# Expert stage of a two-block model: one gather of token rows for two turns, and weight slots handed over in parts

## The reference, cut to what matters

```python
T, D, N_EXPERTS, D_EXPERT, TOP_K = 256, 1024, 32, 512, 2
grp_prob = softmax(hf @ w_group_router + b_group_router)
grp_p, grp_idx = top_k(grp_prob, 1)
exp_logits = (hf @ w_expert_router + b_expert_router).reshape(T, 4, 8)
top_p, top_i = top_k(softmax(exp_logits[grp_idx]), TOP_K)
gates = grp_p * top_p / sum(top_p)
...
def expert_block(xb, e):                 # xb: the rows of the tokens that chose expert e
    hid = silu(xb @ w_expert_gate[e]) * (xb @ w_expert_up[e])
    return hid @ w_expert_down[e]
...
y = segment_sum(yb * row_gate[:, None], row_tok)   # back to the tokens
x = x + y
```

## Time and profile before

| what | us |
|---|---|
| median of 3 runs | 1495.97 |
| the profiled execution, its own time | 1494.68 |
| its span, first to last instruction | 1492.9 |
| first matmul of the first expert turn | 1040.04 |
| last matmul of y in the last turn ends | 1485.97 |

### The profile page before, as it was taken

One profiled execution on the slowest core, in us unless ns is written; L12 is line 12 of the kernel. 1 busy time (PEld: TensorE's weight loads), 2 busy tenths in 40 slices (PEclk: granted clock), 3 DMA queues, 4 the chain that ended last, 5 costly groups with the idle time before them and its releaser, 6 DMA issues.

```text
span 1492.9 us, 20008 instructions
## 1 busy us (share of the span) xinstructions
PE 1444.0 (97%) x7734; PEld 1031.3 (69%) x7734; DVE 638.8 (43%) x1074; ACT 545.6 (37%) x814; POOL 448.6 (30%) x305
## 2 busy tenths in 40 slices
PE   8999999999999999999999999998999899999998
PEld 7788888888788888887878689855454354454453
DVE  6673644446663645434358555644112121212111
ACT  6666544345666534335455421212111111111111
POOL 2472545444463554447679030100000000000000
PEclk9999999999999999999999999999999999999999
DMA  7341454554341454556863601038999999999995
GB/s 270 128 163 57 150 218 170 198 191 142 130 161 58 165 203 169 208 187 202 268 226 104 227 6 57 2 133 374 374 428 428 428 428 428 422 416 422 427 421 242
DMA packets 44675, 351.89 MB, mean 236 GB/s; under 512 B 5187, under 2 KB 7151, under 8 KB 20015
## 3 DMA queue, kind: packets, MB, share of 16 engines
q1 hardware_dynamic: 43758, 349.35, 60.3%
q10 hardware_dynamic: 720, 1.20, 0.2%
q0 software_dynamic: 112, 0.17, 0.1%
HBM read 347.78 MB, written 1.07 MB: 234 GB/s over the span
## 4 chain that ended last, share of the span: by engine, by line
PE 73%; DMA 10%; issue 6%; DVE 5%; ACT 2%; POOL 2%; DVEq 1%; SPq 1%; POOLq 0%; ACTq 0%
PE psum L1743 12%; PE psum L1055 10%; PE psum L1057 10%; PE psum L1056 10%; DMA ring<-in_w_expert_up 9%; PE psum L1347 8%; PE psum L1769 5%; PE psum L1349 4%; PE psum L1045 3%; PE psum L1695 2%; PE psum L1704 1%; PE psum L1176 1%; DMA weights_raw<-in_second_w 1%; PE psum L1562 1%; POOL weights_split L896 1%
## 5 line engine op out<-in xcount | busy, mean ns | idle before, releaser
L896 POOL TENSOR_TENSOR weights_split<-weights_raw,weights_split 128x512 fp32r<-128x512 f32 (+2 forms) x253 | 395.9, 1597 | 360.9 <-ACT weights_split L1844 360.9
L1844 ACT ACTIVATE weights_split<-weights_raw 128x2048 fp32r<-128x2048 f32 (+4 forms) x154 | 243.5, 1586 | 254.6 <-PE psum L1057 150.3
L1743 PE MATMUL psum<-ring,arena 128*64 128x512 f32 x960 | 224.2, 593 | 10.9 <-DMA ring<-in_w_expert_up 9.8
L1347 PE MATMUL psum<-h_split,weights_split 128*128 128x512 f32 x512 | 181.2, 398 | 1.4 <-DVE weights_split L896 1.4
L1743 PEld LDWEIGHTS psum<-ring,arena 128*64 128x64 f32 x960 | 72.9, 137 | 139.8 <-issue 139.8
L1055 PE MATMUL psum<-weights_split,h_split 128*128 128x512 f32 (+3 forms) x400 | 152.0, 380 | 6.3 <-POOL weights_split L896 4.8
L1055 PE MATMUL psum<-weights_split,hidden_split 128*128 128x512 f32 (+1 forms) x384 | 151.4, 394 | 0.0
L896 DVE TENSOR_TENSOR weights_split<-weights_raw,weights_split 128x2048 fp32r<-128x2048 f32 (+3 forms) x53 | 119.5, 2259 | 71.3 <-ACT weights_split L1844 69.4
L1057 PE MATMUL psum<-weights_split,h_split 128*128 128x512 f32 (+3 forms) x400 | 149.9, 375 | 0.0
L1056 PE MATMUL psum<-weights_split,h_split 128*128 128x512 f32 (+3 forms) x400 | 149.8, 374 | 0.0
L1057 PE MATMUL psum<-weights_split,hidden_split 128*128 128x512 f32 (+1 forms) x384 | 148.1, 386 | 0.0
(11 more groups left out here) (379 smaller groups left out, 1928.9 us busy)
## 6 DMA issues: line engine op xcount, KB each, us to landing
weights_raw<-in_layer_w SPq DMA_DIRECT2D x94, 1024.0 KB, 4.8
arena<-in_w_expert_down SPq DMA_DIRECT2D x32, 2048.0 KB, 13.4
ring<-in_w_expert_up SPq DMA_DIRECT2D x32, 2048.0 KB, 16.9
ring<-in_w_expert_gate SPq DMA_DIRECT2D x28, 2048.0 KB, 16.3
weights_raw<-in_second_w SPq DMA_DIRECT2D x44, 512.0 KB, 5.2
arena<-in_w_expert_gate SPq DMA_DIRECT2D x3, 2048.0 KB, 9.5
weights_raw<-in_layer_w SPq DMA_DIRECT2D x6, 768.0 KB, 4.2
ring<-in_w_out SPq DMA_DIRECT2D x2, 2048.0 KB, 17.2
```

Source lines behind the costliest of these rows:

```text
L896: ins = eng.tensor_tensor(W.part(j, 1, n)[:, cols], W.raw(j, n)[:, cols], W.part(j, 0, n).bitcast(F32)[:, cols], ALU.subtract)
L1347: pe.matmul(both.rearrange("p (w s) -> p w s", w=2), w[0][:, k, f * P:(f + 1) * P], hTp[:, :, k, :], start=(k == 0), stop=False)
L1743: ins = pe.matmul(bank[half(j), :], xe[h][:, k, half(j)], w[j][:, k, :], start=(k == 0), stop=(k == KD - 1))
L1844: act.activation(W.part(j, 0, w), W.raw(j, w), ACT.Copy).then_inc(W.hi, 1)
```

## The change

What it does, part by part:

- **Gather.** The normalised rows are kept as two rounded parts, `rows_high` (written by ACT, in the place of `xn2`) and `rows_low` (a new DVE operation per 128 tokens, `low_rows`). `take_pair` has the 0/1 columns of four experts. One gather per two turns makes 32 matmuls of 256 columns in the rounded format (fp32r) into banks 4, 6, 5, 7; it stands behind y of the odd turns. `take_rows` therefore runs once per pair, with 16 small operations instead of 8.
- **Order in a turn.** `give_back` moves ahead of `hT`. y runs over f outside and both output halves c inside, so both halves end together. The gate matmuls of an even turn wait for the gathered rows slice by slice.
- **First gates.** The gates' arithmetic, `gate_tab` and the first `give` move behind the first gather and its copies; the number of turns is computed earlier, right behind the first `take`.
- **First turn's slots.** After each quarter of gate, half of up and quarter of down (`FIRST_PARTS`) TensorE signals `part_done`, and SP loads that part of the next turn's matrices: DMAs of 128 x 1024 or 128 x 2048 float32 instead of 128 x 4096.
- **Last turn's slots.** They are loaded in 2, 2 and 4 parts (`LAST_PARTS`), and TensorE waits for each part where it needs it.
- **Router weights** are loaded by SP in front of the first expert matrix, no longer by POOL.

```diff
+FIRST_PARTS = (4, 2, 4)
+LAST_PARTS = (2, 2, 4)
...
+GATHER_BANKS = (4, 6, 5, 7)
...
-        plan += [(("gate", h), 4, "A"), (("up", h), 5, "V"), (("gx", h, 0), 6, "V"), (("gx", h, 1), 7, "V"),
-                 (("hT", h), 4, "A"), (("gt", h), 6, "A"), (("y", h, 0), 5, "V"), (("y", h, 1), 7, "V")]
-    return plan
+        plan += [(("gate", h), 4, "A"), (("up", h), 5, "V"), (("hT", h), 4, "A"), (("gt", h), 6, "A"),
+                 (("y", h, 0), 5, "V"), (("y", h, 1), 7, "V")]
+    return plan + [(("gx", i), bank, "V") for i, bank in enumerate(GATHER_BANKS)]
...
             for load in loads:
                 units.wait_full(load[-1])
+                if load is loads[0]:
...
+                    sp.dma_start(b_route, row("b_route")).then_inc(route_loaded, 16)
                 if load == ("R", 3, ("rank", T)):
-                    sp.wait_ge(xn2_ready, 1)
+                    sp.wait_ge(xn2_ready, 2)
+                    sp.wait_ge(xn2_low, 2)
...
-            next_matrices(EPT, RoundView(EU, sp, psum, 0), 0)
+            first = RoundView(EU, sp, psum, 0)
+            freed = 0
+            for i, parts in enumerate(FIRST_PARTS):
+                n = SLOT // parts
+                for q_ in range(parts):
+                    if q_ < parts - 1:
+                        freed += 1
+                        sp.wait_ge(part_done, freed)
+                    else:
+                        first.wait_full(stage_of(EPT * i, 0))
+                    for dst, src, s in list(matrices(EPT))[EPT * i:EPT * (i + 1)]:
+                        arrived = part_loaded[i] if q_ < parts - 1 else moe_loaded[s]
+                        sp.dma_start(dst[:, q_ * n:(q_ + 1) * n], src[:, q_ * n:(q_ + 1) * n]).then_inc(arrived, 16)
...
+            for i, parts in enumerate(LAST_PARTS):
+                n = SLOT // parts
+                for q_ in range(parts):
+                    for dst, src, s in list(matrices((TURNS - 1) * EPT))[EPT * i:EPT * (i + 1)]:
+                        if q_ == 0:
+                            wait_slot_free(TURNS - 1, s)
+                        arrived = last_loaded[i][q_] if q_ < parts - 1 else moe_loaded[s]
+                        sp.dma_start(dst[:, q_ * n:(q_ + 1) * n], src[:, q_ * n:(q_ + 1) * n]).then_inc(arrived, 16)
...
-            def gather(i, par):
...
+            def gather(i, bank):
+
+                for kk in range(2):
+                    k = 2 * i + kk
+                    for part, rows in enumerate((rows_high, rows_low)):
+                        for t in range(T):
+                            ins = pe.matmul(bank[:, kk * 2 * P:(kk + 1) * 2 * P], rows[:, t, k * P:(k + 1) * P],
+                                            take_pair[:, t, :, :].rearrange("p j n -> p (j n)"),
+                                            start=(part == 0 and t == 0), stop=(part == 1 and t == T - 1))
...
-                    pe.wait_ge(moe_loaded[s], body * 32 + (16 * h + 16 - 16 * kept_before))
+                    if at is None and h == 1:
+                        pe.wait_ge(part_loaded[s // EPT], 16 * EPT * (FIRST_PARTS[s // EPT] - 1))
+                    if not last:
+                        pe.wait_ge(moe_loaded[s], body * 32 + (16 * h + 16 - 16 * kept_before))
                     return moe_slot[s].rearrange("p (k n) -> p k n", k=k)
...
+                def part_read(i, k, ks, ins):
+
+                    if (k + 1) * FIRST_PARTS[i] % ks == 0 and k + 1 < ks:
+                        ins.then_inc(part_done, 1)
...
-                units.wait_emptied(("gx", 1 - h, 1), 1 - h)
...
                     bank = units.begin((stage, h))
                     for k in range(KD):
+                        if h == 0 and stage == "gate" and k % 2 == 0:
+                            units.wait_emptied(("gx", k // 2), 1)
+                        part_arrived(i, k, KD)
                         for j in range(EPT):
                             ins = pe.matmul(bank[half(j), :], xe[h][:, k, half(j)], w[j][:, k, :], start=(k == 0), stop=(k == KD - 1))
+                        part_read(i, k, KD, ins)
                     units.finish((stage, h), ins)
                 if not last:
-                    pe.wait_ge(take_ready, body * 2 + (2 + h))
-                    for i in range(2):
-                        units.begin(("gx", h, i))
-                        units.finish(("gx", h, i), gather(i, 1 - h))
+                    give_rows_before()
                 units.wait_emptied(("up", h))
...
-                if not last:
-                    give_rows_before()
+                units.finish(("hT", h), ins)
...
                 bank = units.begin(("gt", h))
-                for i, a in enumerate((give[h], take[h])):
+                pe.wait_ge(first_given, 1)
+                for i, a in enumerate((give[h], take[h].bitcast(F32))):
...
-                for c in range(2):
-                    bank = units.begin(("y", h, c))
-                    for f in range(D_EXP // P):
+                banks = [units.begin(("y", h, 0)), units.bank(("y", h, 1))]
+                for f in range(D_EXP // P):
+                    part_arrived(2, f, D_EXP // P)
+                    for c, bank in enumerate(banks):
                         for j in range(EPT):
                             ins = pe.matmul(bank[half(j), :], hidT[:, f, half(j)], w[j][:, f, c * 512:(c + 1) * 512],
                                             start=(f == 0), stop=(f == D_EXP // P - 1))
-                    units.finish(("y", h, c), ins)
+                        if f == D_EXP // P - 1:
+                            units.finish(("y", h, c), ins)
+                    part_read(2, f, D_EXP // P, ins)
+                if h == 1 and not last:
+                    pe.wait_ge(take_ready, body + 2)
+                    for i in range(len(GATHER_BANKS)):
+                        bank = units.begin(("gx", i))
+                        units.finish(("gx", i), gather(i, bank))
...
+            act.activation(rows_high[:, 0, :], x[:, 0, :], ACT.Copy, scale=rstd[:, 0:1]).then_inc(xn2_ready, 1)
...
+            def low_rows(t):
+                dve.wait_ge(xn2_ready, t + 1)
+                dve.scalar_tensor_tensor(rows_low[:, t, :], x[:, t, :], rstd[:, t:t + 1], rows_high[:, t, :].bitcast(F32), mul, sub).then_inc(xn2_low, 1)
...
+            low_rows(0)
...
-            dve.wait_ge(route_exp, 1)
-            dve.tensor_reduce(total, shifted_g, AX.X, add)
...
-            dve.drain()
+            low_rows(1)
...
-            def take_rows(turn, par):
...
+            def take_rows(turn):
+
+                dve.tensor_copy(place_now, place[:, bass.ds(turn * EPT, 2 * EPT), :])
...
-                    for j in range(EPT):
+                    for j in range(2 * EPT):
...
+                for j in range(2 * EPT):
...
             ins.then_inc(take_ready, 1)
+            for q_ in range(1, PASSES):
...
+            dve.sem_inc(turns_ready, 1)
+
+            def gathered(i, bank):
+
+                norm2 = gains2[:, KD + 2 * i:KD + 2 * i + 2].unsqueeze(2).unsqueeze(3).to_broadcast([P, 2, 2, P])
...
+            dve.sem_inc(EU.read["V"], EU.cnt["V"] - len(GATHER_BANKS))
+            for i, bank in enumerate(GATHER_BANKS):
+                dve.wait_ge(first_gathered, i + 1)
+                gathered(i, psum[:, bank, :]).then_inc(EU.read["V"], 1)
+            dve.wait_ge(route_exp, 1)
+            dve.tensor_reduce(total, shifted_g, AX.X, add)
...
+                for j in range(2 * EPT):
+                    ins = dve.tensor_scalar(give[j // EPT][:, t, j % EPT, :], places, place[:, j, t:t + 1], gate_tab[:, j, t:t + 1], ALU.is_equal, mul)
+            ins.then_inc(first_given, 1)
...
-            dve.sem_inc(places_ready, 1)
-            dve.wait_ge(places_ready, 1)
-
-            def gathered(i, par, bank):
...
+            dve.wait_ge(turns_ready, 1)
+
             def turn(body, h, at=None):
                 units, last = RoundView(EU, dve, psum, body), at == TURNS - 1
-                if not last:
-                    units.wait_full(("gt", 1 - h), 1 - h)
-                    take_rows(body * 2 + (1 + h), 1 - h).then_inc(take_ready, 1)
                 bank = units.wait_full(("up", h))
                 units.wait_emptied(("gate", h))
-                dve.tensor_tensor(hid, bank, silu_g, mul).then_inc(EU.read["V"], 3 if last else 1)
-                if not last:
-                    for i in range(2):
-                        bank = units.wait_full(("gx", h, i))
-                        units.emptied_by(("gx", h, i), gathered(i, 1 - h, bank))
+                units.emptied_by(("up", h), dve.tensor_tensor(hid, bank, silu_g, mul))
                 units.wait_emptied(("gt", h))
+                if h == 1 and not last:
+                    units.wait_full(("gt", 1))
+                    take_rows(body * 2 + 2).then_inc(take_ready, 1)
                 for c in range(2):
                     bank = units.wait_full(("y", h, c))
...
+                if h == 1 and not last:
```

(11 more changed lines are left out.)

130 lines of the change are left out of this document (64 added, 66 removed).

## The result

The changed kernel takes 1486.47 us (median of six runs, 1482.52 to 1488.48), against 1494.66 for the kernel before (median of six, 1490.74 to 1497.24): ratio 0.9945, with a 95% interval of 0.9925 to 0.9965, or 8.2 us. The forecast of 1485.5 is 1.0 too low; the 10.5 us it expected between the two kernels lie inside the first interval (5.2 to 11.2), near its better end.

What follows compares the result with a forecast made beforehand. Transfers bound the first half, TensorE narrowly the second. An earlier first load, a cheaper gather and small losses end y 10.6 us earlier, less 0.1 at the end: 1495.97 - 10.5 = 1485.5 us, range 1482.5 to 1491.5.

Steps and rivals of the forecast that it cites:

- The bound: Expert stage: transfers bind the first half, TensorE narrowly the second; relieving one leaves the other 0.7 us a pair behind.
- The sum: Whole chain to the last y: y ends at 1475.4 instead of 1485.97, 10.6 us earlier, giving 1485.5 on the median.
- The start: First turn: first gate matmul at 1040.3 instead of 1040.04, first part issued at 1042.3, bytes flowing 4.9 us earlier.
- The rate of parts: Turn 1's loads: parts of 128 x 1024 run at 414 GB/s, 5.06 us a matrix, losing 1.0 us on six.
- Its range (380, 3.8 lost): Turn 1's loads, mildly slow rival: 380 GB/s, 5.52 us a matrix, 3.8 us lost, 1488.3 us in all; chance 0.12.
- no window under 400 GB/s between 1046 and 1100: Turn 1's loads: a sign the forecast is right, that transfer rates stay at 400 GB/s or more in that stretch.
- The 3.3 us: Up of turn 13: its matmuls begin 3.3 us after the stream brings the matrix, as at up of turn 3 before.
- The Trainium skill: Turn 1's loads: by its 341 GB/s a matrix in parts costs 6.15 us and the six lose 7.5; about 1495.
- The gather: TensorE, once per pair of turns: 32 rounded matmuls take 3.77 us, saving 3.77 a pair; bounds 3.6 and 7.5.
- the hole: TensorE ahead of y, behind `gt`: a gap of 0.46 us in each turn but the last, which had it already.
- The end: Last turn: its parts gain nothing; last part of down lands at 1469.8, its quarter of y begins at 1473.6.
- The clock: TensorE behind up of turn 13: rival that a clock fall after the wait adds 3.3 us, 1488.8; chance 0.08.

Runs made afterwards that it cites:

- gather_only: The changed kernel with the first and last turn's slots loaded whole, so the new gather without parts: 1489.41 us median of six, ratio 0.9972 to the kernel before.
- handover_only: The kernel before with only the first turn's slots handed over in parts and y's halves interleaved: 1492.68 us median of eleven, ratio 0.9995.
- after: The changed kernel itself in its first runs, against the kernel before: 1486.47 us median of six, ratio 0.9945; its profiled execution took 1487.69 us.
- after_again: The changed kernel run once more without an edit: 1486.37 us median of five, ratio 0.9949 to the kernel before.
- gate_halves: The changed kernel with gate of turn 1 handed over in halves instead of quarters: 1485.94 us, one run.
- give_back_split: The changed kernel with half of `give_back` ahead of `hT` and half behind it: 1486.61 us, one run.
- early_split_whole_last: The changed kernel with resident gates in turns 8, 9, 10, 12, `give_back` split around `hT`, and the last turn's slots loaded whole: 1484.01 us, one run.
- early_and_split: The changed kernel with resident gates in turns 8, 9, 10, 12 and `give_back` split around `hT`: 1482.53 us median of six, ratio 0.9923 to the kernel before.
- resident_early: The changed kernel with the resident gates moved to turns 8, 9, 10 and 12 from 8, 10, 12 and 14: 1485.46 us, one run.
- gate_parts_late: The changed kernel with all gate parts of the first turn issued together behind the whole gate stage: 1484.56 us, one run.
- before_again: The kernel before, run once more without an edit: 1495.26 us, one run.

## Why the prediction was right, and where its steps were off

**The bound** was read rightly. Whichever side is relieved alone, the other takes over (gather_only ends in transfers, handover_only in TensorE from turn 9 on), and the second half did become bound by the transfers: 428 GB/s from 1330 to 1360 with 28.3 of 30 us of TensorE, where before had 29.7.

**The sum**, against after's profiled execution, term by term:

| term | predicted | after | after_again |
|---|---|---|---|
| first gate matmul | 1040.3 | 1041.14 | 1039.81 |
| first issue | 1042.3 | 1043.18 | 1041.86 |
| from it to up of turn 13 | 362.8 | 364.70 | 363.08 |
| lost in it against whole matrices | 1.0 | 3.0 | 1.3 |
| of it by the first of the sixteen raises | | 1.8 | 1.4 |
| up of turn 13 to y's end | 70.3 | 70.85 | 70.87 |
| y's end | 1475.4 | 1478.73 | 1475.81 |
| y's end to the span's end | 7.0 | 7.2 | 7.2 |

- *The start.* The issue 2.0 us behind the first gate matmul is right (before it was 7.2). The first gate matmul itself follows the clock at the matmuls ahead of it: in the four kernels with these parts' code and no fall there it comes 13.2 us behind their start, 13.8 in before, and 14.0 where the fall was long, as in after. So `low_rows(1)` (1.28 us, in the range of 0.8 to 1.5) and the longer `take` cost nothing; without a fall the start is 0.6 earlier, not 0.3 later. After's execution had the fall (6.59 us instead of 3.67 in the chain above).
- *The rate of parts* is a term that was mis-sized: 414 GB/s held for the halves of up and the quarters of down (409 to 427 in windows of 4 us), but the gate quarters ran at 328 to 385. Instead of 1.0 they lost 1.4 to 1.8 us, by the first raise. The queue was in fact filled, as the prediction had it; that this makes the rate full was its error. Its range (380, 3.8 lost) held it. Its sign "no window under 400 GB/s between 1046 and 1100" is wrong.
- *The 3.3 us* from the moment at which the stream should have brought a matrix to its first matmul were kept from before without a reason. Most of them is the spread of the sixteen raises (2.4 us at up of turn 3 in before), and it is not the same in two executions of one kernel. After's 3.5 at up of turn 13 against after_again's 2.25 make 1.2 of the 1.6 us between the two.
- The Trainium skill, "DMA: Bandwidth & Descriptors", section "Bandwidth", has 341 GB/s for a 1 MB transfer, issued from GpSimd, and advises batches of at least 1 MiB. For 1 MB loads issued from SP the traces do not agree: they ran at 414 and 434 in gate_halves. The 512 KB quarters did run near its figure for some microseconds (328 to 385 in after), but not with 7.5 us lost: the six matrices of turn 1 had arrived 1.8 us later than whole ones in gather_only.
- *The gather* took 4.01 us, not 3.77; 32 records of 0.125 us instead of 0.118. Once a pair, it is 3.5 us cheaper than two of 3.77. The middle of a turn, 3.19 against 3.22, is right by luck: the hole is 0.25 us (4.0 over 16 turns) and not 0.46, which was read off a last turn whose `hT`, behind a wait of 1.03 us, took 0.67 instead of 0.44, and `give_back` in its new place takes 2.06 instead of 1.88. The gather's 0.24 and 0.22 in up of turn 13, whose matmuls take 7.09 behind a wait, make most of the 0.55 that the last stretch is longer.
- *The end.* "The last turn's parts gain nothing in my sum" is false by 1.26 us. The prediction compared the last quarter of down (1469.8) with its quarter of y (1473.6). It should have set the whole of down, 1469.8, against the start of y, which by its own numbers is 1475.4 - 7.02 = 1468.4: 1.4 late. The sum had the parts in it, so the number didn't suffer.
- *The clock.* The rival of a fall behind up of turn 13 didn't come in the changed kernel: its wait is 1.42 us. Its falls came behind waits of 2.4 and 2.7 us, in the slack of the first half. In the second half the clock did fall in give_back_split (up of turn 11) and early_split_whole_last (up of turn 13).
- *Not settled:* why quarters flow more slowly than halves, why the spread of a load's sixteen raises differs from one execution to the next, and how much of early_and_split's lead over resident_early (1.1 us of stage) is run-to-run.

Where the missing 2.3 us of the median (8.2 of 10.5) are, follows from the stage: predicted 435.1, measured 436.0 and 437.6, or 0.9 to 2.5 too long: 0.3 to 1.9 of it between the first issue and up of turn 13, and 0.55 on TensorE.

## What to carry to other kernels

Where two resources stand about 1% apart, price a change on both at once: relieving one alone hands the time to the other. A slot that is passed on in parts starts its next load earlier, but small parts can lose part of that lead in their rate: here halves did as well as quarters. A wait for a load ends with the last of its sixteen raises; compare two executions by the first as well as by the last before a difference is put down to the edit. And at the end of such a stream compare the whole load with the first use, not the last part with the last use.

## What the runs showed of the hardware

**Rates by the size of the loads.** In windows of 2 us, 512 KB loads handed over two at a time ran at 328 to 385 GB/s in after and 369 to 424 in after_again, and eight issued at once at 406 to 422 (gate_parts_late); 1 MB loads handed over two at a time ran at 414 to 434 (gate_halves), 2 MB loads at 428 over 30 us. The bytes in line do not explain it, as shown under gate_halves.

**Sixteen raises that drift apart.** The first and the last raise of one 2 MB load lie 1.7 us apart in gather_only and 3.7 in after, both at up of turn 3, at the same total rate. In after it then stays between 3.4 and 3.8 us at up of every turn until turn 13. It decides when the wait ends, and it made more of the difference between two executions of one kernel than the rate of the parts did.

**The granted clock behind short waits.** Windows of the changed kernel over the wait of 2.70 us ahead of up of turn 3:

```profile
1126.00:1128.00 2.00, 0.16 (x2) 0.00 (x0) 0.00 (x0) 0.60 (x1) 0.00 (x0) 1.00 1.02 434
1128.00:1130.00 2.00, 1.14 (x4) 0.54 (x6) 0.00 (x0) 0.00 (x0) 0.00 (x0) 0.64 1.00 426
1130.00:1132.00 2.00, 2.00 (x6) 0.49 (x5) 0.00 (x0) 0.00 (x0) 0.00 (x0) 0.50 0.98 418
1132.00:1134.00 2.00, 2.00 (x12) 0.69 (x10) 0.00 (x0) 0.00 (x0) 0.00 (x0) 1.00 1.04 442
```

The clock is at 1.2 instead of 2.4 GHz for some 3 us, and the 32 matmuls take 8.62 us instead of 7.09. This was seen behind waits of 2.4 to 2.8 us in the kernels with the cheap gather, though not behind each of them (up of turn 5 in after waited 2.69 and took 7.09), once behind a single wait of 1.99 us (give_back_split), and behind none of the waits of 1.9 us in before, before_again and handover_only. In gather_only one came behind two short gaps close together, 0.95 and 0.80 us: the last y took 8.78 instead of 7.09.
